# Rows of x moved to multiples of 256 bytes, weight buffers 64 bytes beside one

## The reference

```
xn = rmsnorm(h)
aq, ak, av, agate, iq, ik, iw, cq, ckv, kr, bgate, mg = split_proj(xn @ w_in)      # w_in: 2048 x 9872
o_a = dsa_attend(aq, keys, values, iq, ik, iw)    # indexer, top-k keys, grouped heads
y_a = (o_a * silu(agate)) @ w_o_a
o_b = mla_attend(...)                             # latent attention: w_uq, w_uk, w_uv
y_b = (o_b * silu(bgate)) @ w_o_b
g = sigmoid(mg)
m = g[..., :2048] * y_a + g[..., 2048:] * y_b
h = h + m @ w_out
y = rmsnorm(h) * final_g
```

## Time and profile before

| | |
|---|---|
| time, median of 3 runs | 821.36 us (820.65 to 822.15) |
| time of the profiled execution | 821.64 us |
| its span | 819.9 us |
| TensorE busy with matmuls | 806.9 us, 6276 matmuls |
| TensorE busy with weight loads | 779.3 us |
| VectorE busy | 522.7 us |
| ScalarE busy | 358.3 us |
| granted TensorE clock over the span | 0.997 |
| read from HBM | 134.5 MB, mean 169 GB/s both ways |

### The profile page before, as it was taken

How to read it: one execution, slowest core, us unless ns; L and a number is a source line. 1 busy time by engine, 2 the same in 40 slices (tenths; PEclk the granted TensorE clock), 3 DMA queues, 4 the chain that set the end, 5 groups by cost and what they waited for, 6 DMA issues and landing times.

```text
span 819.9 us, 15423 instructions
## 1 busy us (share of the span) xinstructions
PE 806.9 (98%) x6276; PEld 779.3 (95%) x6276; DVE 522.7 (64%) x845; ACT 358.3 (44%) x528; POOL 49.0 (6%) x56
## 2 busy tenths in 40 slices
PE   7999999999999999999999999999999999999995
PEld 6999999999999998999999999999999999998885
DVE  6798776899876565456544444556466666745665
ACT  7634444453555583244433434343443333334443
POOL 2231102113100000000000000000000000100001
PEclk9999999999999999999999999999999999999998
DMA  9946455544542475134574555455645446474423
GB/s 322 335 148 209 130 163 184 168 134 150 184 124 96 168 246 189 53 104 145 175 245 153 166 183 164 154 156 164 190 128 182 155 153 204 138 288 152 157 104 115
DMA packets 114549, 138.97 MB, mean 170 GB/s; under 512 B 2832, under 2 KB 99744, under 8 KB 113824
## 3 DMA queue, kind: packets, MB, share of 16 engines
q1 hardware_dynamic: 112400, 130.56, 49.1%
q0 software_dynamic: 1808, 7.53, 2.5%
q10 hardware_dynamic: 288, 0.14, 0.1%
HBM read 134.53 MB, written 3.69 MB: 169 GB/s over the span
## 4 chain that ended last, share of the span: by engine, by line
PE 91%; DVE 4%; ACT 2%; issue 1%; DMA 1%; SPq 0%; ACTq 0%; DVEq 0%
PE ps L574 24%; PE ps L575 23%; PE ps L576 23%; PE ps L933 4%; PE ps L937 3%; PE ps L935 3%; PE ps L954 2%; PE ps L784 1%; DVE w_lo L1325 1%; DMA x_t<-in_x_t 1%; PE ps L690 1%; PE ps L756 1%; PE ps L739 1%; PE ps L745 1%; ACT w_hi L996 1%
## 5 line engine op out<-in xcount | busy, mean ns | idle before, releaser
L996 ACT CAST w_hi<-raw 128x1024 fp32r<-128x1024 f32 (+1 forms) x232 | 239.7, 1040 | 322.5 <-PE ps L576 255.4
L1325 DVE TENSOR_TENSOR w_lo<-raw,w_hi 128x1024 fp32r<-128x1024 f32 (+1 forms) x232 | 280.8, 1229 | 153.7 <-ACT w_hi L996 151.9
L574 PE MATMUL ps<-x_hi,w_hi 128*128 128x288 f32 x1232 | 367.1, 298 | 3.6 <-DVE x_lo L1352 2.9
L575 PE MATMUL ps<-x_lo,w_hi 128*128 128x288 f32 x1232 | 363.4, 295 | 0.0
L576 PE MATMUL ps<-x_hi,w_lo 128*128 128x288 f32 x1232 | 363.1, 295 | 0.0
L574 PEld LDWEIGHTS ps<-x_hi,w_hi 128*128 128x128 f32 x1232 | 231.7, 188 | 8.0 <-issue 6.5
L575 PEld LDWEIGHTS ps<-x_lo,w_hi 128*128 128x128 f32 x1232 | 231.7, 188 | 0.2
L576 PEld LDWEIGHTS ps<-x_hi,w_lo 128*128 128x128 f32 x1232 | 231.5, 188 | 0.0
L576 PE MATMUL ps<-og_hi,w_lo 128*128 128x288 f32 x256 | 75.9, 296 | 0.0
L574 PE MATMUL ps<-og_hi,w_hi 128*128 128x288 f32 x256 | 75.7, 296 | 0.0
L575 PE MATMUL ps<-og_lo,w_hi 128*128 128x288 f32 x256 | 74.6, 292 | 0.0
(11 more groups left out here) (263 smaller groups left out, 761.3 us busy)
## 6 DMA issues: line engine op xcount, KB each, us to landing
raw<-in_w_in SPq DMA_DIRECT2D x75, 1024.0 KB, 5.1
raw<-in_w_out SPq DMA_DIRECT2D x16, 1024.0 KB, 5.4
raw<-in_w_o_a SPq DMA_DIRECT2D x8, 1024.0 KB, 5.3
raw<-in_w_o_b SPq DMA_DIRECT2D x8, 1024.0 KB, 5.3
raw<-in_w_uv SPq DMA_DIRECT2D x4, 1024.0 KB, 5.4
raw<-in_w_uq SPq DMA_DIRECT2D x4, 768.0 KB, 4.5
raw<-in_w_ukt SPq DMA_DIRECT2D x2, 1024.0 KB, 5.9
raw<-in_w_uk SPq DMA_DIRECT2D x2, 1024.0 KB, 5.0
```

Of the source, the lines that this page charges most:

```text
L574: nc.tensor.matmul(out, hi, x_h, start=first, stop=False)
L575: nc.tensor.matmul(out, hi, x_l, start=False, stop=False)
L996: nc.scalar.copy(w_hi[:, step % 2, cols], raw[:, step % RAW, cols]).then_inc(hi_done, pieces_done(q))
L1325: nc.vector.tensor_tensor(w_lo[:, step % 2, cols], raw[:, step % RAW, cols], w_hi[:, step % 2, cols].bitcast(F32), ALU.subtract)\
```

## The change

`x_hi` and `x_lo` get rows of 320 numbers (1280 bytes, five times 256), of which 288 are used; `small_t` and `small_u` are put before and behind them, so that `x_hi` begins at 16,640 and `x_lo` at 37,120, multiples of 256, and `raw`, `w_hi` (90,432) and `w_lo` (106,816) lie 64 bytes beside one. `m_hi` and `m_lo` are the same memory as x and get the same rows. All that lies behind moves by 4096 bytes. To make room, `kv_tok` shrinks from 512 to 256 numbers in a row (only the values were ever used), and `y_a` and `y_b` are put over `gate_x`, for which VectorE waits for `gated_lo_done` before the first merge. `at_l` is now written as a sum and goes from 210,528 to 212,448.

```diff
--- before.py
+++ after.py
@@ -30,6 +30,7 @@
 D_MODEL = 2048
 SEQ, DEC, PAST = 256, 32, 256
 NTOK = DEC + SEQ
+ROW = 320
 NKEY = PAST + NTOK
 CHUNK = 64
 EPS = 1e-6
@@ -245,13 +246,14 @@
                 made.append(t)
             return (*made, start)
 
-        (norm_g, x_hi, x_lo, small_t, raw, w_hi, w_lo, ident, ones, rope_tab, lora_g, small_u, x_rstd, o_base) = row(
+        (norm_g, small_t, x_hi_rows, x_lo_rows, small_u, raw, w_hi, w_lo, ident, ones, rope_tab, lora_g, x_rstd, o_base) = row(
             -(-nc.sbuf_base // 64) * 64,
-            ("norm_g_sb", [P, KD]), ("x_hi", [P, KD, NTOK], F32R), ("x_lo", [P, KD, NTOK], F32R), ("small_t", [P, 16]),
-            ("raw", [P, RAW, 2048]),
+            ("norm_g_sb", [P, KD]), ("small_t", [P, 16]), ("x_hi", [P, KD, ROW], F32R), ("x_lo", [P, KD, ROW], F32R),
+            ("small_u", [P, 12]), ("raw", [P, RAW, 2048]),
             ("w_hi", [P, 2, 2048], F32R), ("w_lo", [P, 2, 2048], F32R), ("ident_sb", [P, P]), ("ones", [P, P]),
-            ("rope_sb", [P, 6, NTOK]), ("lora_g", [P, 2, KL]), ("small_u", [P, 12]),
+            ("rope_sb", [P, 6, NTOK]), ("lora_g", [P, 2, KL]),
             ("x_rstd", [P, 1, NTOK]))
+        x_hi, x_lo = x_hi_rows[:, :, 0:NTOK], x_lo_rows[:, :, 0:NTOK]
         ss, var, root, rstd = (small_t[:, 4 * i:4 * i + 4] for i in range(4))
         mx, neg_mx, sum_p, inv_p = (small_u[:, 3 * i:3 * i + 3] for i in range(4))
 
@@ -275,10 +277,12 @@
                                                ("w_iwg", [P, KD, 32]))
         assert d_end <= at_y
 
-        probs_a, probs_ta, aq_t, ka_t, va_past, kv_tok, work, at_l = row(
+        probs_a, probs_ta, aq_t, ka_t, va_past, kv_tok, work, a_end = row(
             at_y, ("probs_a", [P, AHEAD + 2, PAST + DEC]), ("probs_ta", [P, 2, 3, P]),
-            ("aq_t", [P, 8, NTOK]), ("ka_t", [P, A_KV, NKEY]), ("va_past", [P, 2, 256]), ("kv_tok", [P, 3, 512]),
+            ("aq_t", [P, 8, NTOK]), ("ka_t", [P, A_KV, NKEY]), ("va_past", [P, 2, 256]), ("kv_tok", [P, 3, 256]),
             ("work", [P, 3, PAST + DEC]))
+        at_l = at_y + 64 * NTOK + 32 * SEQ + 8 * LORA
+        assert a_end <= at_l
         cq_hi, cq_lo, ckv_tok, iw_tok, top8, iw_four, sel, _ = row(
             at_l, ("cq_hi", [P, KL, NTOK], F32R), ("cq_lo", [P, KL, NTOK], F32R), ("ckv_tok", [P, 3, LORA]),
             ("iw_tok", [P, 3, IDX_HEADS]), ("top8", [P, 2, 8]), ("iw_four", [P, 4]),
@@ -307,9 +311,10 @@
         ckv_old, _ = at("ckv_old", [P, 2, LORA], at_l + 32 * NTOK + 4 * LORA)
 
         merge_g, _ = at("merge_g", [P, 32, NTOK], at_f - 32 * NTOK)
-        og_hi, gate_t, gate_x, y_a, y_b, _ = row(
-            at_y + 64 * NTOK, ("og_hi", [P, 16, NTOK], F32R), ("gate_t", [P, 2, 2, NTOK]),
-            ("gate_x", [P, 2, 2, NTOK]), ("y_a", [P, 2, NTOK]), ("y_b", [P, 2, NTOK]))
+        og_hi, gate_t, at_gate_x = row(
+            at_y + 64 * NTOK, ("og_hi", [P, 16, NTOK], F32R), ("gate_t", [P, 2, 2, NTOK]))
+        gate_x, _ = at("gate_x", [P, 2, 2, NTOK], at_gate_x)
+        y_a, y_b, _ = row(at_gate_x, ("y_a", [P, 2, NTOK]), ("y_b", [P, 2, NTOK]))
         m_hi, m_lo = x_hi, x_lo
 
         h_tok, _ = at("h_tok", [P, 3, D_MODEL], at_f - 32 * NTOK)
@@ -535,7 +540,7 @@
             add_squares(0)
             for tt, (t0, n) in enumerate(TOK):
                 dst = d["new_a_v_sample"] if tt == 0 else d["new_a_v_prompt"][t0 - DEC:t0 - DEC + n, :]
-                pool.dma_start(dst, kv_tok[0:n, tt, 256:512]).then_inc(kv_out, 16)
+                pool.dma_start(dst, kv_tok[0:n, tt, :]).then_inc(kv_out, 16)
             add_squares(1)
             pool.wait_ge(sq_added, 4)
             for group in range(G_AQ, G_FILL_A):
@@ -780,7 +785,7 @@
                             v = vb[:, t - 3, h * P:(h + 1) * P]
                         else:
                             g = h if kind == 0 else h // GRP
-                            v = va_past[:, t, g * P:(g + 1) * P] if t < 2 else kv_tok[:, t - 2, (2 + g) * P:(3 + g) * P]
+                            v = va_past[:, t, g * P:(g + 1) * P] if t < 2 else kv_tok[:, t - 2, g * P:(g + 1) * P]
                         last = nc.tensor.matmul(ps[:, 7, 0:P], v, probs_t[:, u % 2, j, :], start=j == 0,
                                                 stop=j == len(tiles) - 1)
                 last.then_inc(o_ready, 1)
@@ -1083,7 +1088,7 @@
                 if g == G_CQ + 1:
                     for tt, (_, n) in enumerate(TOK):
                         act.wait_ge(tr_ready, 2 + tt)
-                        nc.scalar.copy(kv_tok[0:n, tt, 256:512], ps[0:n, 4 + tt, 0:256]).then_inc(tr_copied, 1)
+                        nc.scalar.copy(kv_tok[0:n, tt, :], ps[0:n, 4 + tt, 0:256]).then_inc(tr_copied, 1)
                 if g == G_CQ + 2:
                     act.wait_ge(idx_added, len(IDX_UNITS))
                     act.wait_ge(idx_out, 16)
@@ -1735,6 +1740,7 @@
                                         ALU.subtract).then_inc(m_done, 1)
                 dve.wait_ge(m_done, j + 1 + 2 * it)
 
+            dve.wait_ge(gated_lo_done, G_END - G_GATE)
             merge_a(0)
             split_lo(STEP_Y + 2)
             merge_b(0)
```

## The result

The changed kernel takes **827.9 us** (median of 4 runs, 827.67 to 828.58) against 821.3 us before on the same chip: a ratio of **1.0083, 95% interval 1.0071 to 1.0096**. It is slower by 0.8%, where 805.8 us had been forecast.

What follows compares the result with a forecast made beforehand. The prediction took TensorE's matmul pitch as the bound: -20.3 (projections) + 4.2 (last stage) + 0.5 (VectorE) = -15.6 us from 821.64 gives 806.0, and 805.8 us as median. Range 794 to 822.5 us, likeliest case 797 to 811.

Steps and rivals of the forecast that it cites:

- Step 1: Projections: 3696 matmuls fall from 132.2 to 126.7 ns through the new placement, 20.3 us saved.
- Step 2: Last stage: 768 matmuls lose their cheap pairing and cost 118.9 ns each, 4.2 us lost.
- Step 3: Output branches: og stays and only the standing w moves, taken as 0, bounds 4.2 us to either side.
- Step 4: The cq, ckv, vb and q_abs products: taken as 0, at most 1.7 us either way.
- Step 5: VectorE from 160 to 210 us: too little idle time to cover faster projections fully, 0.5 us given back.
- Steps 6 and 7: The added gated_lo_done wait costs 0; the copy x_hi<-y_a with wider rows costs 0, at most 0.3 us.
- Step 8: kv_tok, pads and DMA targets 64 bytes off: slightly worse transfers stay hidden at DMA share 0.53, cost 0.
- D: Rival: projections keep 132.2 ns and the last stage loses its good pairing, +4.2 us, 825.6 us; chance 0.14.
- A: Rival: placement does nothing to the matmul, so the time stays at 821.4 us; chance 0.12.
- B: Rival: deeper gain, projections at 123.3 ns, 32.9 us saved there, 794.7 us; chance 0.08 below the forecast range.
- C: Rival: partial gain, say 2.5 ns per projection matmul, 9.2 us saved and 4.2 lost, 816 us; chance 0.12.

Runs made afterwards that it cites:

- x_rows_only: The changed kernel with raw, w_hi and w_lo back at multiples of 256, x rows kept as changed; 823.34 us, ratio 1.0028.
- neither_shift: The changed kernel with x, raw and w placed as before, the rest of the change kept; 820.94 us, ratio 0.9997.
- raw_64_only: As neither_shift, but the load buffers raw alone lie 64 bytes beside a multiple of 256; 822.37 us, ratio 1.0017.
- x_rows_m_apart: As x_rows_only, but m_hi and m_lo lie 64 bytes behind x_hi and x_lo with rows of 1152 bytes; 819.5 us, ratio 0.9983.
- w_192: The changed kernel with raw, w_hi and w_lo 192 instead of 64 bytes beside a multiple of 256; 826.89 us, ratio 1.0068.
- place_grid: Separate kernel, TensorE alone: 24 equal fp32r matmuls at each of 64 placements, 288 then 256 moving columns; mean 132.8 ns with 288.
- sweep_types: Separate kernel, TensorE alone at one placement: 256 to 512 moving columns, fp32r and bf16, 128 and 64 standing columns; bf16 had 6 cycles of excess.
- x_best_m_apart: Against neither_shift: x_hi 256, x_lo 384 bytes beside a multiple of 512, m_hi and m_lo 64 bytes further; 824.22 us, ratio 1.0045.

## Why the prediction was wrong, point by point

- *Step 1, the projections*, is where it failed: "If it is the pair of placements that makes the excess, it goes from 12.2 to the 6.7 ns". It doesn't. A matmul with 288 moving fp32r columns has 28 to 32 cycles of excess at every one of 64 placements, with nothing else running. So of the 5.5 ns by which each of the 3696 matmuls was to get cheaper nothing came: the excess went from 12.2 to 13.3 ns. The last stage is cheap because it moves 256 columns and, at that number, happens to have a distance at which the rhythm of 272 cycles holds. I had the row that should have warned me: ckv with 256 columns and 118.9 ns hints that 256 columns react to placement; that 288 do so alike was shown by none, and the og rows, at other places, had the same 12.2 ns as x. The 20.3 us saved became 3.9 us lost, as the new distance is one of those with 320 cycles for rows of 1280 bytes.
- *Step 2, the last stage*: the direction was right, the size too large. 4.2 us was forecast, 1.4 measured, since only every other stretch of 96 matmuls ran in the slower rhythm. That the pairing of before was lost, and at about the price of ckv's row (282.7 cycles against 285), was right. That row was taken because its moving operand lies off a multiple of 256, and this isn't what counts: in x_rows_only w lies at one, and the stage has 285.4 cycles, 4.1 us more than neither_shift.
- *Step 3, the output branches*: taken as 0, was 0.9 us dearer, inside the bounds. The ground (w is moved, og isn't) was right and should have been given its price: the distance changes for every partner of w.
- *Step 4, the small products*: taken as 0, and under 0.3 us together.
- *Step 5, VectorE*: as TensorE became no faster, it was never tested. VectorE is busy for 47.7 of 50 us from 160 to 210, as before.
- *Steps 6 and 7*: borne out by neither_shift (820.94 us) and by the copy x_hi<-y_a, which still takes 0.45 us (L1738 after).
- *Step 8, the loads*: "so a slightly worse transfer stays hidden" took the DMA share of the projections from 420 us on, 0.53. From 20 to 40 us the share was 1.00 before, and there it isn't hidden: raw_64_only lost 1.4 us.
- *The rivals*: D came nearest, with the right sign, the number of columns as the source of the cheap stage, and a dearer last stage, but it kept the projections at 132.2 ns. No case had them dearer, and so none reached 827.9. A was right in that placement doesn't remove the excess, wrong in that it does nothing. B and C had gains in the projections; the most that any run showed over the whole stage is 1.3 cycles (0.5 ns), in x_rows_only and x_rows_m_apart.
- *The rules*: the Trainium skill ("TensorE: Matmul & The Clock Gate", section "Part 2: What happens when you issue a matmul") has two independent read ports, and the prediction read from this that placement would change nothing. The grid shows 316 to 320 cycles with 288 columns and 272 to 288 with 256, so the measurement decides against that reading for fp32r. The same page of the Trainium skill (section "Back-to-back issue gap") gives N/2.4 + 2.5 ns, there for isolated matmuls; back to back it is met by bf16, 294.0 cycles (122.5 ns) for 288 columns, and not by fp32r, 131.7 ns at the least in the grid.

Left open: what in the chip turns a distance into these steps, what decides between two rhythms at one placement and ends the 312 in the kernel, and the 2.6 cycles of w_192's output branches.

## What to carry to other kernels

When one stage is cheaper than another, list all that differs between them, and price a change only from a row that has the same number of columns, or measure the one suspected cause by itself first: a kernel of bare matmuls over a grid of placements costs one run, and it told the projections' pitch within 0.3 cycles. It also told where two rhythms are possible, but not which one the kernel would fall into. Moving a buffer that every matmul reads changes the distance to every partner, and moving one that loads land in changes the loads: look for the stretch where the DMA engines have no pause, not at their mean. Where one memory serves two stages in different roles, give each role its own offset, if a few bytes are free.

## What the runs showed of the hardware that was not expected

- fp32r matmuls with 288 moving columns and 128 standing ones start 316.0 to 320.3 cycles apart at 2.4 GHz, bf16 ones 294.0, with no other engine at work (place_grid, sweep_types). With both operands at 0 the excess of fp32r is 24 cycles with 64 standing columns and 28 with 128; at 256 moving columns it is 16 and 32.
- The distance between the moving row and the standing tile, modulo 256 bytes mostly, moves the pitch between 316 and 320 cycles (288 columns) and between 272 and 288 (256 columns). At some placements two rhythms are possible, and a stretch of matmuls keeps the one it is in: 272.6 and 282.7 cycles by turns in the last stage of the changed kernel, 312.0 and then 320.0 in the projections of x_best_m_apart.
- Loads of 1024-byte rows that land 64 bytes beside a multiple of 256 moved 333 instead of 344 GB/s in a stretch in which the DMA engines were busy all the time, with 51 instead of 46 ns for a packet.
